# Eight stage heads of a fused transformer kernel: products with the operand's high part first, those with its low part one step of features later

## The reference

```python
def hybrid_layer(x, ...):                       # block 1, once
    h = rmsnorm(x, norm1_w)
    proj = h @ w_in
    ...                                         # dilated attention, gated linear attention, block attention
    x = x + mix @ w_out
    h2 = rmsnorm(x, norm2_w)
    x = x + jnp.square(jax.nn.relu(h2 @ w_ff1)) @ w_ff2

for l in range(DEPTH_2):                        # block 2, two layers
    hx = modulate(rms_norm(x, norm1_g[l]), sh1, sc1)        # and the same for the context
    px = hx @ w_in[l]
    ...                                         # latent attention, Fourier mixing, long convolution
    x = x + g1 * heads_out(att_x, px, hy, w_out[l])
    x = x + g2 * sq_relu_mlp(modulate(rms_norm(x, norm2_g[l]), sh2, sc2), w_mlp1[l], w_mlp2[l])
```

## Time and profile before

| | |
|---|---|
| median of 3 runs | 2536.83 us (2532.84, 2536.83, 2537.53) |
| the profiled execution | 2532.73 us, of which the span is 2530.9 us |
| PE busy | 2366.2 us, 93% of the span |
| PEld, DVE, ACT, POOL busy | 72%, 57%, 36%, 22% |
| mean granted PE clock | 0.97 |
| PE products on line 600 with `mix_split` (3792) | 786.7 us |
| PE products on line 600 with `normed_in` (1080) | 218.9 us |

### The profile page before, as it was taken

How to read it: one execution, slowest core, us unless ns; L and a number is a source line. 1 busy time by engine, 2 the same in 40 slices (tenths; PEclk the granted TensorE clock), 3 DMA queues, 4 the chain that set the end, 5 groups by cost and what they waited for, 6 DMA issues and landing times.

```text
span 2530.9 us, 29291 instructions
## 1 busy us (share of the span) xinstructions
PE 2366.2 (93%) x11174; PEld 1833.2 (72%) x11174; DVE 1434.0 (57%) x2277; ACT 905.1 (36%) x1539; POOL 564.3 (22%) x431
## 2 busy tenths in 40 slices
PE   6999999999998997888899999999899988999998
PEld 4665567888876864657788888888676566788886
DVE  4465547888757446665465566544636674534435
ACT  4244444232233223774332222222421773423232
POOL 2523114122211222002131211211123002322221
PEclk9999899999999999999899999999899999999999
DMA  5411114555521321001043334431122112222321
GB/s 185 150 53 42 55 34 175 200 179 188 175 79 34 107 67 52 27 22 47 30 133 123 127 128 132 127 103 62 50 89 83 34 34 67 84 92 92 102 90 50
DMA packets 77910, 234.06 MB, mean 92 GB/s; under 512 B 9215, under 2 KB 12416, under 8 KB 77772
## 3 DMA queue, kind: packets, MB, share of 16 engines
q1 hardware_dynamic: 70928, 217.48, 26.4%
q0 software_dynamic: 3520, 11.58, 1.3%
q10 hardware_dynamic: 3324, 3.14, 0.4%
HBM read 224.26 MB, written 7.90 MB: 92 GB/s over the span
## 4 chain that ended last, share of the span: by engine, by line
PE 86%; DVE 7%; ACT 3%; issue 2%; POOL 1%; ACTq 0%; DVEq 0%; POOLq 0%
PE psum L600 38%; PE psum L870 24%; PE psum L639 4%; PE psum L1168 3%; PE psum L1199 2%; PE psum L1125 2%; PE psum L659 2%; PE psum L1183 1%; PE psum L776 1%; PE psum L747 1%; PE psum L571 1%; PE psum L558 1%; PE psum L1139 1%; PE psum L1061 1%; DVE mla_stat L2007 1%
## 5 line engine op out<-in xcount | busy, mean ns | idle before, releaser
L600 PE MATMUL psum<-mix_split,weight_split 128*128 128x512 f32 x3792 | 786.7, 368 | 14.2 <-DVE mix_split L1316 5.9
L600 PEld LDWEIGHTS psum<-mix_split,weight_split 128*128 128x128 f32 x3792 | 651.0, 190 | 149.4 <-issue 17.7
L870 PE MATMUL psum<-hidden,weight_split 128*128 128x512 f32 (+1 forms) x3072 | 630.6, 366 | 0.0
L870 PEld LDWEIGHTS psum<-hidden,weight_split 128*128 128x128 f32 x3072 | 522.8, 188 | 104.4
L2086 ACT CAST weight_split<-weight_ring 128x1024 fp32r<-128x1024 f32 x269 | 276.8, 1040 | 301.2 <-PE psum L870 232.2
L2619 POOL TENSOR_TENSOR weight_split<-weight_ring,weight_split 128x1024 fp32r<-128x1024 f32 x89 | 233.9, 2628 | 541.3 <-ACT weight_split L2086 540.8
L1638 DVE TENSOR_TENSOR hidden<-hidden_tmp,hidden 128x512 fp32r<-128x512 f32 (+1 forms) x128 | 156.1, 1240 | 318.5 <-POOL hidden_tmp L2752 318.5
L2752 POOL TENSOR_TENSOR hidden_tmp<-hidden_tmp 128x512 f32<-128x512 f32 (+1 forms) x128 | 125.8, 994 | 615.1 <-ACT hidden L2331 614.9
L1262 DVE TENSOR_TENSOR weight_split<-weight_ring,weight_split 128x1024 fp32r<-128x1024 f32 x180 | 228.4, 1271 | 53.6 <-ACT weight_split L2086 53.6
L2327 ACT ACTIVATE hidden_tmp<-psum 128x512 f32<-128x512 f32 (+1 forms) x128 | 69.0, 539 | 494.9 <-PE psum L600 494.9
L600 PE MATMUL psum<-normed_in,weight_split 128*128 128x512 f32 (+1 forms) x1080 | 218.9, 364 | 9.0 <-DVE normed_in L1316 6.9
(11 more groups left out here) (303 smaller groups left out, 2415.6 us busy)
## 6 DMA issues: line engine op xcount, KB each, us to landing
weight_ring<-in_w_mlp SPq DMA_DIRECT2D x128, 512.0 KB, 3.8
weight_ring<-in_w_ff SPq DMA_DIRECT2D x64, 512.0 KB, 4.7
mod_ring<-in_w_mod SPq DMA_DIRECT2D x48, 512.0 KB, 3.8
late_ring<-in_w_mod SPq DMA_DIRECT2D x96, 256.0 KB, 3.5
weight_ring<-in_w_in SPq DMA_DIRECT2D x45, 512.0 KB, 3.7
weight_ring<-in_w_out SPq DMA_DIRECT2D x24, 512.0 KB, 3.6
weight_ring<-in_tables SPq DMA_DIRECT2D x13, 512.0 KB, 3.5
weight_ring<-in_w_v SPq DMA_DIRECT2D x8, 512.0 KB, 4.1
```

The lines of the kernel that those rows point to most:

```text
L600: m = pe.matmul(psum[:, b + r, 0:hi - lo], w[:, part_w, :], x[:, part_x, k, lo:hi], start=k == 0 and part_w + part_x == 0, stop=k == KT - ...
L870: mm = pe.matmul(psum[:, b + r, 0:hi - lo], w[:, part_w, :], G[:, part_x, f % (2 * GROUP), lo:hi], start=jj == 0 and part_w + part_x == 0, ...
```

## The change

`product` gets a second body for calls with an `x_ready`; it now returns two steps for each k, that of the high part and that of the low one. For each k from 0 to 8, PE waits for the high part of tile k and issues (0,0) and (1,0) for both output tiles, then waits for the low part of tile k-1 and issues (0,1) for both. So all products with the low part stand one k later. Calls without an operand to wait for pass `None` and keep the old body. What is computed, and the number of instructions on every engine, stay the same; the programs of DVE, ACT, POOL and SP are unchanged.

```diff
+                if x_ready:
+                    for k in range(KT + 1):
+                        if k < KT:
+                            pe.wait_ge(*when(*x_ready(k)[0]))
+                        for parts, kk in ((((0, 0), (1, 0)), k), (((0, 1),), k - 1)):
+                            if not 0 <= kk < KT:
+                                continue
+                            if parts == ((0, 1),):
+                                pe.wait_ge(*when(*x_ready(kk)[1]))
+                            for (i, _), b, load in zip(tiles, bs, at):
+                                j = split_at[load]
+                                w = WS[:, j % SPLIT_RING, :, kk * P:(kk + 1) * P]
+                                if kk == 0 and parts[0] == (0, 0):
+                                    pe.wait_ge(*when(lo_of(j), j))
+                                    wait_bank(*range(b, b + len(ranges)))
+                                for part_w, part_x in parts:
+                                    for r, (lo, hi) in enumerate(ranges):
+                                        m = pe.matmul(psum[:, b + r, 0:hi - lo], w[:, part_w, :], x[:, part_x, kk, lo:hi],
+                                                      start=kk == 0 and part_w + part_x == 0, stop=kk == KT - 1 and part_x == 1)
+                                if kk == KT - 1 and part_x == 1:
+                                    m.then_inc(*did("gemm", (tag, i)))
...
+                    return
                 for k in range(KT):
...
-                        for name, key in x_ready(k):
-                            pe.wait_ge(*when(name, key))
...
-                x_ready = lambda k: [("n1_pool" if k % 2 else "n1_vec", ("lo", k, 0))]
+                x_ready = lambda k: (("n1_act", ("hi", k, 0)), ("n1_pool" if k % 2 else "n1_vec", ("lo", k, 0)))
...
-                    product("out1", [(i, ("w_out1", i))], HS_T1, X1, lambda k: (), lambda i, r: ("out1_vec", ("add", i, r)))
+                    product("out1", [(i, ("w_out1", i))], HS_T1, X1, None, lambda i, r: ("out1_vec", ("add", i, r)))
```

More of the change, by code:

```diff
@@ L588, in product @@
                 at = [use_load(*w, split=True) for _, w in tiles]
+                if x_ready:
[19 more added lines that the diff above has]
+                                    m.then_inc(*did("gemm", (tag, i)))
+                                    split_use[j] = (tag, i)
+                                    for r in range(len(ranges)):
+                                        freed[b + r] = [evac(i, r)]
+                    return
                 for k in range(KT):
@@ L851, in mlp @@
                         for fs in ([(0, 1), (2,), (3,)] if g == 0 else [(g * GROUP + j,) for j in range(GROUP)]):
-                            x_ready = (lambda k: [(norm_tag + ("_pool" if k % 2 else "_vec"), ("lo", k, len(ranges) - 1))]) if fs == (0, 1) else (lambda k: ())
+                            last = len(ranges) - 1
+                            x_ready = (lambda k: ((norm_tag + "_act", ("hi", k, last)), (norm_tag + ("_pool" if k % 2 else "_vec"), ("lo", k, last)))) if fs == (0, 1) else None
                             product(tag + "_up", [(f, w1(f)) for f in fs], HS, ranges, x_ready,
@@ L945, in in_projection_2 @@
                 evac = lambda i, r: in2_evac(l, i, r)
-                x_ready = lambda k: [(norm_tag + ("_pool" if k % 2 else "_vec"), ("lo", k, 1))]
+                x_ready = lambda k: ((norm_tag + "_act", ("hi", k, 1)), (norm_tag + ("_pool" if k % 2 else "_vec"), ("lo", k, 1)))
                 product(tag, [(i, ("w_in2", (l, IN2[i][0]))) for i in range(2)], HS_2, in2_span(l, 0), x_ready, evac)
                 for i in range(2, 14):
-                    product(tag, [(i, ("w_in2", (l, IN2[i][0])))], HS_2, in2_span(l, i), lambda k: (), evac)
+                    product(tag, [(i, ("w_in2", (l, IN2[i][0])))], HS_2, in2_span(l, i), None, evac)
                     next(filt, None)
@@ L1227, in block_2 @@
                 for ms in [(0, 1)] + [(i,) for i in range(2, KT)]:
-                    x_ready = (lambda k: [(f"mix2_{l}" + ("_pool" if k % 2 else "_vec"), ("lo", k))]) if ms == (0, 1) else (lambda k: ())
+                    x_ready = (lambda k: ((f"mix2_{l}_act", ("hi", k)), (f"mix2_{l}" + ("_pool" if k % 2 else "_vec"), ("lo", k)))) if ms == (0, 1) else None
                     product(f"out2_{l}", [(i, ("w_out2", (l, i))) for i in ms], HS_T2, RG, x_ready, lambda i, r: (f"out2_{l}_vec", ("add", i, r)))
```

## The result

The changed kernel takes 2524.38 us, the median of 6 runs (2522.68 to 2527.67), beside 2537.18 us of the kernel before (6 runs, 2532.47 to 2541.98). The ratio is 0.9947, with a 95% interval of 0.9935 to 0.9959: 0.5% faster, which is 12.8 us by the medians and 13.5 by the ratio. The profiled execution took 2522.68 us, with a span of 2520.7, against 2532.73 and 2530.9 before.

The account below looks back on a forecast made before the run. PE was taken to bound the kernel (86% of the chain), with tile 0's low part on the path at head starts. Head gains of 3.3 us plus 1.7 for the clock took 5.0 from 2535.0: 2530.0 us, range 2525.5 to 2536.0.

Parts of the forecast that it names:

- The start moves by what lies between the two parts: At the heads, PE's start moves from low part's end to high part's: 0.72, 0.99 (`out2_0`) or 1.36 us earlier.
- `in2_1` gains nothing: At the end of `in2_1`, PE waits for POOL's low weights of the third tile: gain 0, wait up to 1.4 longer.
- `mlp2_1` is bound by DVE's low weights: At the end of `mlp2_1`, the third tile's low weights end at about 2168.0; gain 0.35 us (0.3 to 0.9).
- The convolution behind `in2_0` hangs on tile 0: Behind `in2_0`, tile 0 completes 0.70 us later against the head's end, so 1.07 us shrinks to 0.37.
- The one step of the clock at `out2_1`: Behind the start of `out2_1`, the 3.41 us stretch at 0.50 should not come: 1.7 us of work.
- No waits that cost anything inside the heads: Inside the heads no gap opens and unmet waits cost nothing; the other end was 1.1 us.
- rival 4: At the heads, PE waits between high parts and the clock rises later: slower, 2543.6 us; chance 0.05.
- rival 3: Heads are hidden as `in2_1` is; only `out2_0` and `mlp2_0` keep their gain, 1.2 us, 2533.8; chance 0.11.
- a start that moves forward inside a stretch at 0.50, whose end stays, gains half: At half-clock heads, half the shift arrives: `in1` 0.36, `mlp1` 0.36, `out2_0` 0.50, `mlp2_0` 0.68 us.
- The rule of the Trainium skill: At the heads, activity releases the throttle, so the clock's rise moves with the start: whole shifts, 5.5 us in sum.
- In the other heads ... I leave the clock as it was: Outside `out2_1`, PE had been idle or short of work for longer, so no clock change was counted.
- Rival 2: The clock rises one stretch earlier at more heads, 1.7 us each: about 8 us, 2527; chance 0.22.

Follow-up runs that it names:

- e1: The change, but the first product also waits for the low part of tile 0, as before: 2535.5 us, ratio 0.9991 to the kernel before.
- e3: New body only in the three 768-column heads `in2_0`, `out2_0`, `mlp2_0`, old order and wait elsewhere: 2525.2 us, ratio 0.9957 to the kernel before.
- e4: New body only in `in1`, `mlp1`, `in2_1`, `out2_1`, `mlp2_1`, old order and wait elsewhere: 2530.48 us, ratio 0.9982 to the kernel before.
- e8: The kernel before, unchanged, run once for a second profile: 2533.38 us, span 2531.4.
- e2: The change, but low-part products of tile k right behind its high-part ones, without the lag of one k: 2523.26 us, ratio 0.9952 to the kernel before.
- e7: The change, with the last two steps of `in2_0` made for output tile 0 first, then tile 1: 2523.81 us, ratio 0.9952 to the kernel before.
- e9: The change, unchanged, run again for a second profile: 2525.32 us, ratio 0.9951 to the kernel before.
- e10: The kernel before, plus two or three unread products per head between the high and low part of tile 0: 2531.39 us, ratio 0.998.
- e5: The kernel before, plus 118 unread products filling PE's idle time in norms and at heads except `in1`: 2519.99 us, ratio 0.9931.
- e6: The change, plus 90 unread products filling PE's idle time in norms and at heads except `in1`: 2514.79 us, ratio 0.992 to the kernel before.

## Why the prediction was wrong in size and right in direction

Each head was measured from PE's last instruction of the norm or the attention to the first product of the third tile (to the last but one of the fourth tile for `in2_0`), by the starts of instructions in the profiles: three or four with the old head and four or five with the new one, from among before, e1, e3, e4, e8 and the change, e2, e3, e4, e7, e9. e1 has the old start but the new order, so it is left out of `in2_0` and `mlp2_1`, where the order counts; e7 is left out of `in2_0`.

| head | old, us | new, us | gain | predicted |
|---|---|---|---|---|
| `in1` | 16.8 (16.3 to 17.5) | 16.2 (15.6 to 16.7) | 0.6 | 0.36 |
| `mlp1` | 17.1 | 15.6 (16.67, four times 15.4) | 1.5 | 0.36 |
| `in2_0` | 44.5 (44.0 to 45.3) | 44.5 (43.8 to 45.2) | 0 | 0.37 |
| `out2_0` | 22.1 | 20.36 | 1.76 | 0.50 |
| `mlp2_0` | 22.4 | 21.1 | 1.3 | 0.68 |
| `in2_1` | 18.86 | 18.85 | 0 | 0 |
| `out2_1` | 15.53 | 13.20 | 2.33 | 0.72 + 1.7 |
| `mlp2_1` | 17.35 | 16.94 | 0.41 | 0.35 |
| sum | | | 7.9 | 5.0 |

What held, by its steps:
- The start moves by what lies between the two parts. Held, and up to 0.1 us more: behind PE's last instruction of the norm or attention the first product comes 0.82 us earlier in `mlp1` and `out2_1`, 1.08 in `out2_0` and 1.44 in `mlp2_0`, against 0.72, 0.99 and 1.36.
- `in2_1` gains nothing. PE starts 0.05 us behind POOL's end (1806.95 + 2.36 = 1809.31, and 1809.36) and idles 1.58 there instead of 0.63.
- `mlp2_1` is bound by DVE's low weights: PE starts on them after 0.17 us of waiting. The gain of 0.41 fits the 0.35, and it is the order's: e1, with the old start, has 16.97.
- The convolution behind `in2_0` hangs on tile 0, and tile 0's later end costs 0.70: PE's wait for the residual is 2.48 to 2.49 us in three profiles with the old head and 3.18 to 3.19 in four with the new one; e7 took back 1.05. Whether the start's own gain arrives hangs on the clock. In the first profile of the change the ACT step came 21.19 us behind PE's last instruction of the norm, before 21.42, so 0.23 earlier with 0.4 foretold. In e9 and e2 it came after 22.47 and 22.39, since there the clock was at 0.50 for 5.8 and 5.6 us behind the start. On the mean nothing is left of the 0.37.
- The one step of the clock at `out2_1`: 2.33 measured, 2.4 foretold. By the profiles of e1 and e10 the time at which PE becomes active decides it, with or without useful work.
- No waits that cost anything inside the heads. The one of 0.35 us in `in2_1`, a gap that the first profile of before hadn't, lies in front of a longer one. So rival 4 is out, and rival 3 as well, since in `mlp1`, `out2_0` and `mlp2_0` PE still runs 192 to 384 products without a break.

What failed is the step "a start that moves forward inside a stretch at 0.50, whose end stays, gains half". The end does not stay.
- `mlp2_0`: its start moved by 1.44 us. Had the rise stayed, the head would be at 0.50 for 2.94 + 1.44 = 4.38 us; it was for 3.48. Over all profiles the rise comes 2.9 to 3.9 us behind the old start and 3.5 behind the new one, so it moved with the start, and the head gained 1.3 instead of 0.68.
- `out2_0`: the rise comes 2.9 to 3.0 us behind the start in the new profiles and 4.2 to 5.3 in the old ones (4.2 in e1), though the start is about 1 us earlier. Here the rise moved further than the start, and the gain is 1.76, more than the whole shift. e10, with the same activity but the useful work only from the low part on, keeps 4.66 us at 0.50: what else must hold for the earlier rise, the runs don't show.
- `mlp1`: four of five new profiles have the rise about 3 us behind the start. The first profile of the change has it after 6.21, and by it alone the step would have seemed right: from the norm to the third tile 0.40 shorter, as foretold.
- `mlp2_1`: here the rise came later, 5.8 to 5.9 us behind the start in four new profiles and 2.9 to 3.1 in the old ones. It cost nothing there, since the third tile waits for its weights: e4, with 3.2 us, has the same 16.94.

The rule of the Trainium skill that stood beside the sum ("TensorE: Matmul & The Clock Gate", "What's actually happening") has the rise follow the activity; `mlp2_0` agrees with it, in `out2_0` the rise moved further than the start, and in `mlp2_1` it came later. It would have given 5.5 us, nearer than the step that I preferred but still under half of the result. The spread of 2.8 to 6.1 us in one trace should have told that the rise isn't fixed to the start either.

The second failure is in "In the other heads ... I leave the clock as it was". The forecast took the clock to be the same everywhere but in the heads. Between them the mean of the profiles is about 3 us shorter, in stretches whose code is the same:
- `in2_0` to `out2_0` (the rest of layer 0's mixer and its attention): 351.0 to 354.0 us in four old profiles, 350.8 to 351.05 in five new ones, 1.3 on the mean.
- `in2_1` to `out2_1`: 268.75, 266.57 and 269.08 with the old wide heads, 266.54 to 266.60 in all profiles with the new ones and no other addition. With old wide heads in e4 and in e10 it was 270.04 and 268.87. That is 2.0 on the mean of the first three and e4. The two profiles of before alone show that this is no work of the change: 268.75 and 266.57 with one and the same code.
- `in1` to `mlp1` 0.5 shorter, which rests on one profile (340.67 us in e2, 343.4 to 344.5 in all others); behind `mlp2_1` 0.6 longer; the other four stretches together 0.3 longer.

With the heads that makes 7.9 + 1.3 + 2.0 + 0.5 - 0.6 - 0.3 = 10.8 of the 12.8 us. One us of the difference between the first two profiles is no work of the change: PE's first instruction of all came at 20.25 us before and at 19.17 after, behind the transfers of the inputs; in e8 and e9 it came at 19.77 and 19.84.

The two profiles of each kernel give the account another side. PE's idle time in them, the span less its busy time, is 164.7 and 164.5 us before, 154.7 and 154.9 now: 9.8 us less. Its busy time, where a lower clock would show, is 2366.2 and 2366.9 before, 2366.0 and 2368.3 now. In these four executions the earlier starts arrive whole, and the clock gives and takes about the same. But the two of before, 2532.73 and 2533.38 us, are among the shortest of their kernel, and lie only 9.1 us above those of the change. What the longer executions of the kernel before spend their further us on, no profile of it shows; the clock of the runs says that half of the 12.8 us goes with it.

Rival 2 ("The clock gives more", 8 us, chance 0.22) came nearest, and was still too small, since it counted rises in heads only and was capped. The base was low too: 2535.0 was taken, and the medians of before later were 2536.9 to 2538.8. This hid a part of the miss: 5.0 us from the median of 2537.2 would have read 2532.2, further off.

What stays open: why layer 0's attention takes 351 us in some profiles and 353 to 358 in others (357.6 to 357.9 in e5, e6 and e10), why the stretch in front of `out2_1` keeps one length with the new wide heads and changes with the old ones, and what sets how far the rise lies behind a start. All are seen in the profiles and no run separates their cause. The shares of idle time and clock in the 12.8 us are estimates.

## What to carry to other kernels

Where PE has rested before a stage, count how early it becomes active there and not only how much work moves. The same order was worth some 13 us here, some 3 to 5 (with a wide interval) where the clock was higher already, and e1 took nearly all of it back by delaying one product per head. When a change moves such a start, compare the busy time of untouched stages in two or three profiles of each kernel before a us is put down to the changed lines. And where short rests of PE come again and again, filling them with products that nobody reads was worth 17 us of 2537 here, at least about as much as the reordering.

## What the runs showed of the hardware

- PE's first product came 0.04 us after ACT's high part when that released it, and 0.14 after DVE's low part (`mlp1`, `mlp2_0` and `out2_1` after; the earlier trace rows). In e1, where PE waits for both, one behind the other, it came 0.10 after the low part in `mlp1`. That is up to 0.1 us a head that the forecast didn't have.
- The stretch at 0.50 behind the start of `mlp1` was 6.21 and 3.15 us long in two executions of one kernel that started it 2.3 us apart. In the unchanged part of layer 1 the same 1094 or 1095 instructions were busy for 242.8 to 242.9 us in three of the profiles shown and for 244.8 to 244.9 in two, with nothing in between.
- Behind the start of `in1` the profile's clock reads 1.00, but the first products of 512 columns start 0.43 us apart, where a product at full clock takes 0.233, and only the later ones 0.23: 6 such products in the first profile of before, 13 in e3 and e4. The prediction counted this start at half, and here that can't be checked by the clock shown.
- 24 runs of the kernel before, beside e1 to e4, spread from 2527.08 to 2542.11 us, with a mean granted clock of 0.973 in the fastest and 0.967 in the slowest.
